# Two output mixers: router logits in four column groups of TensorE, and the first mixer's bias added to the residual on GpSimd

## The reference, cut to what matters

```
x = x + _grid_pos_embed(rows, D_MODEL)[None]
...
yl = z @ w_out + b_out                                   # first block (_hyena)
x = _ln_affine(DEEPNORM_ALPHA * x + (1.0 + m_l[2]) * yl, ln_g[i, 0], ln_b[i, 0])
hl = _modulate(x, m_l[3], m_l[4])
...
x = x + m_lat[2][:, None] * mix_lat                      # second block, mix_lat = ... @ w_out
h_lat = modulate(rms_norm(x, norm2_g[l]), m_lat[3], m_lat[4])
...
aff = jax.nn.softmax((h @ w_router), -1)                 # both: 16 logits for each token
gate, idx = lax.top_k(jnp.swapaxes(aff, 1, 2), cap)
```

## Time and profile before

| what | us |
|---|---|
| median of 3 runs | 4224.52 (4223.45 to 4225.65) |
| span of the profiled execution | 4222.7 |
| out1: first projection product to last bank read (profile) | 996.8 to 1127 |
| out1: DVE alone (profile) | 1127 to 1143.7 |
| out1: transposes, then logits (profile) | 1143.7 to 1154.6 to 1168.5 |
| out1: softmax and top tokens (profile) | 1168.5 to 1202 |
| out2: logits (profile) | 3759.6 to 3773.6 |

### The profile page before, as it was taken

The page is one execution under the profiler, slowest core; times in us unless marked ns, Lnnn a source line. Parts: engine busy times, 40 slices in busy tenths (PEclk is TensorE's granted clock), DMA queues, the critical chain, the costliest instruction groups (busy, mean ns, idle before and its releaser), DMA issues. The chain is left out here.

```text
span 4222.7 us, 48091 instructions
## 1 busy us (share of the span) xinstructions
PE 3766.0 (89%) x19722; PEld 2097.9 (50%) x19722; DVE 1514.2 (36%) x2605; ACT 702.1 (17%) x1496; POOL 456.0 (11%) x521
## 2 busy tenths in 40 slices
PE   4999989988869999999999997999776997778995
PEld 1444478874324444444444444544454987333442
DVE  4666369983520000000000003453084777241003
ACT  1000012211110100010001002321135443011111
POOL 0000000002000000000000001000031874200110
PEclk8999999998979999999999998999887999888997
DMA  6556332314169888888988884321202001219995
GB/s 268 205 220 238 155 120 110 130 50 190 70 232 326 308 305 311 307 309 308 312 308 310 300 307 175 119 80 66 105 1 75 4 4 39 112 50 346 341 333 178
DMA packets 283535, 815.53 MB, mean 193 GB/s; under 512 B 10945, under 2 KB 18425, under 8 KB 268118
## 3 DMA queue, kind: packets, MB, share of 16 engines
q1 hardware_dynamic: 263066, 720.11, 47.2%
q0 software_dynamic: 19168, 82.08, 5.9%
q10 hardware_dynamic: 1116, 10.71, 0.6%
HBM read 718.21 MB, written 94.66 MB: 192 GB/s over the span
## 5 line engine op out<-in xcount | busy, mean ns | idle before, releaser
L1285 PE MATMUL banks<-moe_ring,moe_xeT 128*128 128x512 f32 x2560 | 1129.7, 594 | 6.9 <-ACT moe_xeT L1326 6.9
L1285 PEld LDWEIGHTS banks<-moe_ring,moe_xeT 128*128 128x128 f32 x2560 | 481.9, 191 | 584.6 <-issue 581.8
L1379 DVE TENSOR_TENSOR moe_hid<-moe_silu,banks 128x512 f32<-128x512 f32 x80 | 55.0, 688 | 1429.2 <-PE banks L1285 1429.2
L1271 PE MATMUL banks<-moe_ring,moe_hidT 128*128 128x512 f32 x1280 | 562.6, 592 | 1.7 <-DVE moe_ye L1365 1.0
L1271 PEld LDWEIGHTS banks<-moe_ring,moe_hidT 128*128 128x128 f32 x1280 | 240.8, 190 | 293.4 <-issue 291.3
L1594 PE MATMUL banks<-hT,w_in_ring 128*128 128x512 f32 (+3 forms) x976 | 364.1, 535 | 1.7 <-ACT hT L1666 0.9
L434 PE MATMUL banks<-hT,w_in_ring 128*128 128x512 f32 x768 | 341.8, 600 | 3.7 <-ACT hT L456 3.7
L1594 PEld LDWEIGHTS banks<-hT,w_in_ring 128*128 128x128 f32 (+1 forms) x976 | 183.2, 188 | 180.7 <-issue 170.3
L1345 ACT ACTIVATE moe_silu<-banks 128x512 f32<-128x512 f32 x80 | 47.8, 597 | 1302.7 <-PE banks L1285 1302.7
L434 PEld LDWEIGHTS banks<-hT,w_in_ring 128*128 128x128 f32 x768 | 143.2, 191 | 193.8 <-issue 180.3
L969 PE MATMUL banks<-w_out,mix 128*128 128x512 f32 x512 | 226.3, 600 | 7.0 <-DMA w_out<-d_w_out 5.9
(11 more groups left out here) (425 smaller groups left out, 3965.1 us busy)
## 6 DMA issues: line engine op xcount, KB each, us to landing
moe_ring<-d_wg SPq DMA_DIRECT2D x80, 2048.0 KB, 8.1
moe_ring<-d_wu SPq DMA_DIRECT2D x80, 2048.0 KB, 8.2
moe_ring<-d_wd SPq DMA_DIRECT2D x80, 2048.0 KB, 7.9
x_normed<-d_ada_w SPq DMA_DIRECT2D x12, 2048.0 KB, 11.9
w_in_ring<-d_w_in SPq DMA_DIRECT2D x9, 2048.0 KB, 10.4
x_normed<-d_mod_w SPq DMA_DIRECT2D x8, 2048.0 KB, 14.5
d_taps<-dft SPq DMA_DIRECT2D x8, 2048.0 KB, 7.4
taps_in<-d_taps SPq DMA_DIRECT2D x8, 2048.0 KB, 9.4
```

Of the source, the lines that this page charges most:

```text
L1271: last = nc.tensor.matmul(m.ps[:, Y_BANK + h, :], hidT[:, c, i * P:(i + 1) * P], down(c)[:, i, h * BANK:(h + 1) * BANK], start=(fc == 0 an ...
L1285: last = nc.tensor.matmul(m.ps[:, 2 * kind + c, :], xeT[:, k, :], up(c, kind)[:, k, :], start=(k == 0), stop=(k == KT - 1))
L1379: nc.vector.tensor_tensor(hid[:, j % 2, :], sg[:, j % 2, :], m.ps[:, 2 + j % 2, :], ALU.mult).then_inc(s.hid, 1)
```

## The change

The bias becomes a tile of 128 equal rows. Its load is a broadcast, DVE scales it once by gate / ALPHA, and POOL adds it to each tile of x + pos, so that ALPHA * x later carries gate * bias. The ninth product of each group is gone. PE no longer waits for the parameters ahead of the projection, in either mixer; it waits for the router just ahead of the logits.

For the logits the router tile holds each slice twice, side by side (32 columns), loaded by two DMAs. The tokens are split in four groups u of 256 (token tiles u and u + 4). Each slice k makes four products of 256 tokens, each in its own 32 columns of the array and its own 32 partitions of one bank. ACT copies [128, 256], PE transposes that in two pieces, and DVE picks the first 16 of each 32 columns.

```diff
@@ sync
-            sp.dma_start(router[:], d_router).then_inc(s.params, 16)
-            sp.dma_start(flip[:], m.dram["flip"]).then_inc(s.params, 16)
+            for j in range(2):
+                sp.dma_start(router[:, :, j, :], d_router).then_inc(s.router_in, 16)
+            sp.dma_start(flip[:], m.dram["flip"]).then_inc(s.router_in, 16)
...
-                sp.dma_start(bias[:], m.dram["b_out"]).then_inc(s.params, 16)
+                sp.dma_start(bias[:], m.dram["b_out"][0].partition_broadcast(P)).then_inc(s.bias_in, 16)
@@ gpsimd
-                    nc.gpsimd.tensor_tensor(m.X[:, t, :], m.X[:, t, :], xh[:, t, :], ALU.add).then_inc(s.sum, 1)
+                    nc.gpsimd.tensor_tensor(m.X[:, t, :], m.X[:, t, :], xh[:, t, :], ALU.add).then_inc(s.part, 1)
+                    if t == 0:
+                        pool.wait_ge(s.biased, 1)
+                    pool.wait_ge(s.part, t + 1)
+                    nc.gpsimd.tensor_tensor(m.X[:, t, :], m.X[:, t, :], bias[:], ALU.add).then_inc(s.sum, 1)
@@ tensor
-            pe.wait_ge(s.params, 80 if deep else 32)
...
-                                                stop=(k == KT - 1 and not deep))
-                    if deep:
-                        last = nc.tensor.matmul(m.ps[:, 2 + g % 4, :], m.ones[0:1, :], bias[:, h * BANK:(h + 1) * BANK],
-                                                start=False, stop=True)
...
-            for h in range(HALF):
-                for k in range(KT):
-                    if h == 0:
-                        pe.wait_ge(s.hT, 2 * k + 2)
-                    last = nc.tensor.matmul(m.ps[0:E, h, :], router[:, k, :], hT[:, k, h * BANK:(h + 1) * BANK],
+            pe.wait_ge(s.router_in, 48)
+            for k in range(KT):
+                pe.wait_ge(s.hT, 2 * k + 2)
+                tiles = hT[:, k, :].rearrange("p (h u c) -> p u h c", h=2, c=P)
+                for u in range(TT // 2):
+                    last = nc.tensor.matmul(m.ps[32 * u:32 * u + 32, 0, 0:2 * P].rearrange("p (h c) -> p h c", h=2),
+                                            router[:, k].rearrange("p a e -> p (a e)"), tiles[:, u],
                                             start=(k == 0), stop=(k == KT - 1))
...
-            for t in range(TT):
-                last = nc.tensor.transpose(m.ps[:, 2, t * E:(t + 1) * E], logits[:, t * P:(t + 1) * P], m.ident[0:E, 0:E])
+            for h in range(2):
+                last = nc.tensor.transpose(m.ps[:, 2, h * P:(h + 1) * P], logits[:, h * P:(h + 1) * P], m.ident[:])
@@ scalar
-            nc.scalar.copy(logits[:], m.ps[0:E, 0:2, :].rearrange("p a b -> p (a b)")).then_inc(s.logit, 1)
+            nc.scalar.copy(logits[:], m.ps[:, 0, 0:2 * P]).then_inc(s.logit, 1)
@@ vector
-                v.wait_ge(s.params, 80)
+                v.wait_ge(s.bias_in, 16)
+                nc.vector.scalar_tensor_tensor(bias[:], bias[:], 1.0 / ALPHA, gr[:], ALU.mult, ALU.mult).then_inc(s.biased, 1)
+                v.wait_ge(s.params, 32)
```

More of the change, by code:

```diff
@@ L893, in mixer_out_stage @@
     spent = [] if deep else [sem for sem in m.signals if sem not in m.ahead]
-    s = signals(nc, name, "pos sum params diag gate_mm gate out_mm out_read var std var2 std2 xhat stored summed tr_mm "
+    s = signals(nc, name, "pos part bias_in biased sum params router_in diag gate_mm gate out_mm out_read var std var2 std2 xhat stored summed tr_mm "
                           "hT logit_mm logit lt_mm smax sexp aff at_mm aff_row top ix_mm ix flip_mm cols x vec",
@@ L901, in mixer_out_stage @@
         nc.sbuf_tensor(f"{name}_ln", [P, 2, D], F32) as ln,
-        nc.sbuf_tensor(f"{name}_bias", [1, D], F32) as bias,
+        nc.sbuf_tensor(f"{name}_bias", [P, D], F32) as bias,
         nc.sbuf_tensor(f"{name}_tmp", [P, 2, BANK], F32) as tmp,
@@ L905, in mixer_out_stage @@
         nc.sbuf_tensor(f"{name}_stat", [P, 4, 2 * TT], F32) as stat,
-        nc.sbuf_tensor(f"{name}_router", [P, KT, E], F32) as router,
-        nc.sbuf_tensor(f"{name}_logits", [E, T], F32) as logits,
+        nc.sbuf_tensor(f"{name}_router", [P, KT, 2, E], F32) as router,
+        nc.sbuf_tensor(f"{name}_logits", [P, 2 * P], F32) as logits,
         nc.sbuf_tensor(f"{name}_aff", [P, TT // 2, 2, E], F32) as aff,
@@ L969, in _ @@
                         last = nc.tensor.matmul(m.ps[:, 2 + g % 4, :], m.mixT[:, k, t * P:(t + 1) * P],
-                                                w[:, k, h * BANK:(h + 1) * BANK], start=(k == 0),
-                                                stop=(k == KT - 1 and not deep))
-                    if deep:
-                        last = nc.tensor.matmul(m.ps[:, 2 + g % 4, :], m.ones[0:1, :], bias[:, h * BANK:(h + 1) * BANK],
-                                                start=False, stop=True)
+                                                w[:, k, h * BANK:(h + 1) * BANK], start=(k == 0), stop=(k == KT - 1))
                     last.then_inc(s.out_mm, 1)
@@ L1106, in _ @@
             v.wait_ge(s.lt_mm, 1)
-            lt = m.ps[:, 2, 0:TT * E].rearrange("p (t e) -> p t e", e=E)
+            lt = m.ps[:, 2, 0:2 * P].rearrange("p (t e) -> p t e", e=2 * E)[:, :, 0:E]
             by_tile = aff[:].rearrange("p u h e -> p h u e")
```

## The result

The changed kernel takes 4179.81 us (median of 4 runs, 4178.25 to 4182.06); the kernel before took 4223.99 in the same runs (4220.39 to 4225.65). The ratio is 0.9896, interval 0.9885 to 0.9908. Its profiled execution has a span of 4176.5 us, 46.2 less than before. The prediction of 4183.8 with a range of 4178 to 4193 holds; 4179.81 lies 4.0 under it, and 0.2 under the forecast's own range of 4180 to 4189. The gain is 44.2 by the medians and 46.2 by the spans, against 40.7 forecast.

The account below looks back on a forecast made before the run. TensorE, busy 89% of the span, was taken to bound projection and logits, VectorE the top-token search. Terms -20.0 - 0.7 + 1.0 - 2 x 10.3 - 2 x 0.65 + 0.9 = -40.7 gave 4183.8 us, range 4178 to 4193.

Parts of the forecast that it names:

- The bias product: First mixer's projection: dropping the ninth product shortens each of 16 groups from 8.11 to 6.87 us, -20.0 us.
- The early start: First mixer: the projection no longer waits 1.07 us for the bias load; -0.7 us, bounds 0 to 1.4.
- VectorE: First mixer's projection: VectorE, taking turns with GpSimd's 16 additions, closes the last bank late; +1.0 us, bounds 0 and 6.
- The logits: Router logits: four column groups work at once, 3.4 us in place of 13.7; -10.3 us in each mixer.
- Behind the logits: From ACT's copy of the logits to the exponential: shorter copy and fewer transposes, -0.65 us in each mixer.
- The loads: Second mixer: the split router's short-row loads delay the projection's weights, +0.9 us, bounds 0.3 and 2.6.
- VectorE further behind: Rival, chance 0.15: in the first mixer x and pos start later or GpSimd adds slower; 3 to 8 us more, 4187 to 4192.
- the weight loads: Rival, chance 0.10: in the logits, weight loads don't overlap at 256 columns; 3.8 us more, 4187.6.
- the column groups: Rival, chance 0.06: in the logits, the column groups run one after another; 20.6 us less gain, 4204.4.
- GpSimd holding the stage: Rival, chance 0.02: slower than before, with first-mixer additions of 6 us, 47 late against 41.7 gained; 4230.
- The whole greater gain: Rival, chance 0.04: full early projection start, no VectorE lateness, no load delay; 4181.5 or some less.

Follow-up runs that it names:

- The runs with an earlier GpSimd: Changed kernel with router and flip loads issued last (4180.46 us); also gate products behind the first projection group (4176.99); also norm broadcasts behind x and pos (4176.17).
- the third addition: Changed kernel with the first mixer's bias halved and added twice per tile, so GpSimd makes 24 additions; 4194.66 us, ratio 0.9929.

## Why the prediction was right

**The bias product.** Right in mechanism and size. In out1 after, DVE's first bank read starts at 1004.34 and its sixteenth at 1107.26: 15 groups in 102.92 us, 6.86 a group where 8.11 stood. 16 times 1.25 is 20.0. The run with the bias part alone gives the same 21 us by the last read, with the early start.

**The early start.** The sum took 0.7; the projection started 1.27 earlier, and 1.0 of it arrived at the last read (21.01 less the 20.0). That was inside the bounds of 0 to 1.4. But what the removed wait is worth in the changed kernel is another number. With the wait kept, the split router and the broadcast bias would have made it 5.5 us long, and the kernel 8 us slower at the last read, as the run with the wait put back shows. The old wait of 1.07 was a wait for loads that the same change makes later. The sum had the right answer for the change as a whole; for the wait as an edit of its own 0.7 would have stood where 8.0 was measured. That 0.7 and the measured 1.0 lie close holds for these edits together only.

**VectorE.** The mechanism held, the size of the term did not: +1.0 was counted and DVE was not late at all. Counted were closes at 1027, 1033, 1047, 1063, 1077, 1087, 1097.5 and 1108.0; DVE's closes (L1062) started at 1027.98, 1034.24, 1049.18, 1065.25, 1076.50, 1086.83, 1097.15 and 1107.99. GpSimd's last addition was counted to end at 1070 and ended at 1069.5. That the last four agree within 0.5 is luck, since the counts were made from a stage that began at 990.22 and this one began 1.5 us later, at 991.76. Counted from the stage's start, the first four closes lie within 0.7 us of the count, and the last four came 1.5 to 2.0 us earlier than counted. Two things made that: GpSimd started 31.3 us into the stage, where 32.3 was counted, and the fifth tile took 11.25 us, where 14 was counted. DVE had 0.43 us to spare. The runs with an earlier GpSimd (28.9, 28.8, 25.6) show that this changes no read, and the third addition shows how near the edge it was.

**The logits.** 3.4 was counted and 3.7 measured, from PE's start to ACT's copy, against 13.94: a gain of 10.2 in each mixer, where 10.3 stood. By starts four products take 0.217 us, so the bound of 0.215 was met; the 0.3 more lie between the last product's start and ACT's copy. The rule of the Trainium skill ("TensorE: Matmul & The Clock Gate", Part 3, Packing small matmuls), by which weight loads overlap only with products of another row group, would have given 5.4; the trace does not agree with it here. PE's weight loads in out2 after:

```profile
3724.11 3.18 PEld L992 LDWEIGHTS banks<-mix,out_router 128*32 128x32 f32 x64 [0.17 <-issue]
3724.11 3.66 PE L992 MATMUL banks<-mix,out_router 128*32 128x256 f32 x64
```

The loads are busy 3.18 us within the same 3.66 in which the products run, so they lie beside them. The kernel before could have told it: in its projection, where the eight products of a group use all rows, PE was busy 129.89 us and PEld 51.99 within the same 130.20.

**Behind the logits.** -0.72 and -0.73 measured, -0.65 counted. The table load was what ended last, and not the transposes, as the lower of the two counts had it (1.67 for 1.69).

**The loads.** Here the mechanism was half right. The sum took +0.9 between 0.3 and 2.6 on the ground that data on the way cover part of a slower landing; +1.0 came at the last read (+1.5 at the start). The runs showed that landing has little part in it: the weights' products start 8.8 to 9.1 us after the weights' issue in all four kernels looked at. 1.2 of the 1.5 are SP's time to issue what stands ahead of the weights, and 0.3 are the difference between 9.12 and 8.81, of which no run shows the cause. The lower bound, named "the longer issue alone" at 0.3, should have been 1.2. The rows of the profile before did not show a short-row issue of this shape.

**What the sum had not.** Small terms of the clock. In out1, PE's transposes to the logits took 10.27 in place of 10.83 (-0.56), and the transposes of the scores behind the softmax 1.89 in place of 1.05, at a granted clock of 0.80 on average there, so that the search began 0.43 later (1.05 is PE's L1001 in the kernel before, 1172.15 us; the window of the changed kernel is below).

```profile
1138.30:1142.30 4.00, 1.55 (x8) 1.01 (x9) 1.40 (x6) 1.92 (x3) 0.00 (x0) 0.80 0.00 0
```

Neither is a property of the change: with the wait back and with the third addition, both on top of the change, these marks stood at 10.70 and 10.64, and the search began as early as before. Together they are -0.1. With -42.2 in the two mixers for -40.7 predicted, the difference is the lateness that didn't come (1.0) and the pieces above; the other 2 to 4 us of the measured gain are in the rest of the table.

**The rivals.** VectorE further behind fell with 0.43 us of idle left, the weight loads and the column groups with the 3.66, GpSimd holding the stage with additions of 2.9 us where 5.6 would decide. The whole greater gain (4181.5) came nearest by its total, but not for its reason: the lateness was missing, but the start gave 1.0 and not 1.4, the loads did cost 1.0, and 2 to 4 us lie in stages that the change doesn't touch. GpSimd's 16 additions took 46.5 us from first to last with their turns, where the prediction's count had 47.5.

## What to carry to other kernels

When the output of a product uses few columns of the array, put independent token groups into different column groups; here four products took about the time of one, and making the products smaller alone gave nothing. A one-row product that adds a bias costs more than its own records, so a bias that another idle engine can add ahead of time is nearly free, as long as the turns that the engine takes from VectorE fit in VectorE's slack; count them tile by tile. When a change makes loads longer, look at every wait that stands on them: removing the wait may be worth more than its length in the old profile.

## What the runs showed of the hardware that was not expected

- Behind idle times of 2.88, 5.51, 5.27 and 7.41 us at the starts of the stages, PE started again at the lower level of the clock (0.50); behind the 1.07 of the kernel before, its first group went at full pace (16 records in 7.13 us). So a wait near the start of a stage can cost more than its length: 1.8 us longer went with 4.8, and 5.7 with 8.0, in one execution each. Starting sooner gives back only about half: 2.1 gave 1.2, and 1.7 gave 0.9. The time at which the clock rises differed by 2 to 3 us between executions of the same code.
- Loads of short rows (64 bytes, 1024 of them) cost SP's time at the issue: 1.29 us for two where one of whole rows took 0.33, and flip's issue behind them took 0.65 in place of 0.42. The products that need the weights behind them still start 8.8 to 9.1 us after the weights' issue.
- The stages that are the same in all eleven kernels differ by up to 7 us from one profiled execution to another, while a stage's own marks repeat better: the last read of out1 stands at 115.42, 115.43, 115.50 and 115.50 in four kernels, with one at 116.58 for the clock. Differences of 2 us can be read from marks, not from totals.
